# Scan of a two-layer diffusion trunk on one core: TensorE's order per group, fewer loads at the opening, and first output weights split in pieces

## The reference, cut to what matters

```python
    v = _bidir_long_conv(v * x1, h_fwd, h_bwd, f_bias)
    return (v * x0) @ out_w
```

```python
    y_diag = jnp.einsum('bclsgr,bcsgrp->bclgrp', cb[..., None] * decay, xdt)
    ...
    y_off = jnp.einsum('bclgn,bcgrpn->bclgrp', cm, starts) * jnp.exp(a_cum)[..., None]
    y = (y_diag + y_off).reshape(b, length, SSD_HEADS, SSD_HEAD_DIM)
    ...
    y = y_f + _flip(y_b) + d_skip.astype(jnp.float32)[:, None] * xh
    y = y.reshape(b, length, SSD_D_INNER) * jax.nn.silu(z.astype(jnp.float32))
    y = _rmsnorm(y, norm_g).astype(h.dtype)
    return y @ out_w, s_f, s_b
```

## Time and profile before

| | us |
|---|---|
| median of 3 runs | 3874.42 (3873.01 to 3878.49) |
| profiled execution | 3875.18 |
| its span, first to last instruction | 3873.4 |
| Hyena output, first to last product of TensorE | 851.0 to 987.3 |
| scan, first load issued to last residual | 2476.2 to 2946.0 |

### The profile page before, as it was taken

One profiled execution on the slowest core, in us unless ns is written; L12 is line 12 of the kernel. 1 busy time (PEld: TensorE's weight loads), 2 busy tenths in 40 slices (PEclk: granted clock), 3 DMA queues, 4 the chain that ended last, 5 costly groups with the idle time before them and its releaser, 6 DMA issues. The chain is left out here.

```text
span 3873.4 us, 58285 instructions
## 1 busy us (share of the span) xinstructions
PE 3469.3 (90%) x23815; PEld 2919.6 (75%) x23815; DVE 1830.3 (47%) x3029; ACT 1279.6 (33%) x2042; POOL 368.3 (10%) x355
## 2 busy tenths in 40 slices
PE   4999898979499999997899999589996499999996
PEld 2999643448399999996799999455555499999995
DVE  6233366555533333333444555678885533333333
ACT  4223312024133333333333223356665133333332
POOL 0000000000011111111010000000000011111111
PEclk6999899989699999998899999799997699999998
DMA  6556302055588888885143443676664488888885
GB/s 227 177 199 209 136 11 73 0 180 174 182 293 291 291 284 284 286 292 164 52 140 104 149 155 110 218 267 228 223 229 153 157 291 293 290 284 284 288 292 197
DMA packets 412727, 789.78 MB, mean 204 GB/s; under 512 B 22071, under 2 KB 107772, under 8 KB 412299
## 3 DMA queue, kind: packets, MB, share of 16 engines
q1 hardware_dynamic: 384012, 701.15, 51.4%
q0 software_dynamic: 28368, 86.61, 7.8%
q10 hardware_dynamic: 208, 0.10, 0.0%
HBM read 678.89 MB, written 108.90 MB: 203 GB/s over the span
## 5 line engine op out<-in xcount | busy, mean ns | idle before, releaser
L2017 PEld LDWEIGHTS moe_banks<-moe_xt,mix_ring 128*128 128x128 f32 x8192 | 1012.3, 191 | 5.5 <-issue 3.2
L2017 PE MATMUL moe_banks<-moe_xt,mix_ring 128*128 128x144 f32 x8192 | 1013.6, 287 | 3.1 <-ACT moe_xt L2052 3.1
L62 PE MATMUL ssdin_banks<-h_leading,ssdin_w_split 128*128 128x384 f32 x1920 | 412.0, 344 | 0.0
L2039 PE MATMUL moe_banks<-moe_down_parts,moe_hid_parts 128*128 128x512 f32 x1536 | 357.6, 392 | 0.0
L2097 DVE TENSOR_TENSOR moe_hid<-moe_banks,moe_sg 128x128 f32<-128x128 f32 x256 | 74.6, 292 | 581.8 <-ACT moe_sg L2075 581.8
L62 PEld LDWEIGHTS ssdin_banks<-h_leading,ssdin_w_split 128*128 128x128 f32 x1920 | 337.1, 188 | 14.4 <-issue 13.6
L2039 PEld LDWEIGHTS moe_banks<-moe_down_parts,moe_hid_parts 128*128 128x128 f32 x1536 | 285.8, 188 | 71.4 <-issue 13.2
L2087 DVE TENSOR_TENSOR moe_down_parts<-mix_ring,moe_down_parts 128x2048 fp32r<-128x2048 f32 x128 | 292.2, 2283 | 0.0
L2975 PE MATMUL scan_banks<-scan_w,scan_yc 128*128 128x512 f32 x576 | 256.5, 599 | 0.0
L62 PE MATMUL hyin_banks<-h_leading,hyin_w_split 128*128 128x384 f32 x1152 | 238.2, 338 | 11.5 <-DVE hyin_w_split L751 11.5
L1984 POOL DMA_INDIRECT x_dram<-moe_yc,mix_idx_quarter x128 | 167.6, 1309 | 809.3 <-DVE moe_yc L2108 780.1
(11 more groups left out here) (412 smaller groups left out, 4368.8 us busy)
## 6 DMA issues: line engine op xcount, KB each, us to landing
mix_ring<-in_moe_w_gate SPq DMA_DIRECT2D x64, 2048.0 KB, 7.8
mix_ring<-in_moe_w_up SPq DMA_DIRECT2D x64, 2048.0 KB, 12.7
mix_ring<-in_moe_w_down SPq DMA_DIRECT2D x64, 2048.0 KB, 15.8
early_ring<-in_ada_w SPq DMA_DIRECT2D x96, 512.0 KB, 5.8
scan_cum<-row_dram SPq DMA_DIRECT2D x36, 1024.0 KB, 6.3
ssd_w<-in_ssd_in_w SPq DMA_DIRECT2D x40, 512.0 KB, 4.1
scan_states<-s_dram SPq DMA_DIRECT2D x36, 512.0 KB, 7.6
s_dram<-ssdin_work SPq DMA_DIRECT2D x64, 256.0 KB, 2.0
```

What stands on the lines that cost most here:

```text
L62: ins = pe.matmul(out(piece), w_at(w[a], k), h_k(h[b], k, piece), start=(k == 0 and a == 0 and b == 0), stop=(k == KD - 1 and a == 1))
L2017: ins = pe.matmul(pb[:, 2 * (f % 2) + j, 0:SLOTS], ring[:, 2 * half + j, k, col:col + P], xt[:, k, :], start=(k == 0), stop=(k == KD - 1))
L2039: ins = pe.matmul(pb[:, LAT_BANK[half], :], hid_parts[:, a, k, :], wd[:, half, b, k, :], start=(k == 0 and a + b == 0), stop=(k == KD - 1 ...
```

## The change

In the scan TensorE's round becomes: the states' products of n, `cb(n + 1)`, `project(n - 1)`, the mixing products of n. Since two sets of products that lie apart in time now add to the same PSUM bank, each group first writes zeros to the whole bank by a product of one row of zeros (`y_open`), and all others only add. The row of zeros is copied once by ScalarE. The states of tile 0 are no longer loaded (they aren't used), so the group's semaphore counts 48 for the first four groups. The gate and x tile 0 are issued behind the load of group 6, gate and x tile 1 behind that of group 8. In the Hyena output each weight half is prepared in four pieces of two k rows; TensorE waits for each piece of the second half apart.

```diff
@@ phase_hyena_out
+        W_PIECES = 4
+        def weight_piece(half, piece):
+            return slice(2 * piece, 2 * piece + 2), slice(half * HALF, (half + 1) * HALF)
         def lead_count(t):
-            return t + 3 if t else 2
+            return 2 * W_PIECES + t + 1 if t else W_PIECES + 1
...
                     act.wait_ge(s_w[half], 16)
-                    act.activation(w_parts[:, 0, :, cols], w[:, :, cols], ACT.Copy).then_inc(s_hi, 1)
+                    for piece in range(W_PIECES):
+                        ks, cols = weight_piece(half, piece)
+                        act.activation(w_parts[:, 0, ks, cols], w[:, ks, cols], ACT.Copy).then_inc(s_hi, 1)
...
-                    elif t == 0:
-                        pe.wait_ge(s_lo, 3)
                     for k in range(KD):
+                        if t == 0 and half and k % 2 == 0:
+                            pe.wait_ge(s_lo, piece_count(1, k // 2))
...
@@ phase_scan
-                    sp.dma_start(sg[:, r, :, :], io["s_dram"][max(t, 1), :, g, :, :]).then_inc(s_in[r], 16)
+                    if t:
+                        sp.dma_start(sg[:, r, :, :], io["s_dram"][t, :, g, :, :]).then_inc(s_in[r], 16)
...
-                    if n == 3:
-                        for c in range(2):
-                            sp.dma_start(gate[:, c, :], io["vec_dram"][1, c, V_G1:V_G1 + 1, :].partition_broadcast(P)
-                                         ).then_inc(s_gate, 16)
-                        load_x(0)
-                        load_x(1)
+                    if n in (6, 8):
+                        c = CTX if n == 6 else LATENT
+                        sp.dma_start(gate[:, c, :], io["vec_dram"][1, c, V_G1:V_G1 + 1, :].partition_broadcast(P)
+                                     ).then_inc(s_gate, 16)
+                        load_x(n // 2 - 3)
...
+                def y_open(n):
                     if n >= 2:
                         pe.wait_ge(s_yk, 4 * (n - 1))
+                    pe.matmul(pb[:, y_bank(n), :], zero[0:1, :], zero[0:1, :].unsqueeze(1).broadcast_to([1, 4, P]),
+                              start=True, stop=False)
...
+                def y_states(n):
+                    t, r, b = n // GROUPS, n % RING, n % 2
+                    y_open(n)
+                    if t:
+                        pe.wait_ge(s_ce, n - GROUPS + 1)
+                        y_terms(n, [(sg[:, r, d, :], ec[:, b, d * GH:(d + 1) * GH, :]) for d in range(2)], False)
+                def y_mix(n):
+                    r, b = n % RING, n % 2
+                    pe.wait_ge(s_mix, n + 1)
+                    y_terms(n, [(xdt[:, b, d, :], cum[:, r, d, :, :]) for d in range(2)], True).then_inc(s_y, 1)
...
                 for n in range(N + 2):
                     if n < N:
-                        y(n)
+                        y_states(n)
                     if n + 1 < N:
                         cb(n + 1)
                     if 1 <= n <= N:
                         project(n - 1)
+                    if n < N:
+                        y_mix(n)
```

More of the change, by code:

```diff
@@ L1448, in phase_hyena_out, with piece_count @@
         s_cur = m.sem("affinities_cleared")
+        W_PIECES = 4
+        def weight_piece(half, piece):
+            return slice(2 * piece, 2 * piece + 2), slice(half * HALF, (half + 1) * HALF)
         def lead_count(t):
-            return t + 3 if t else 2
+            return 2 * W_PIECES + t + 1 if t else W_PIECES + 1
+        def piece_count(half, piece):
+            return half * (W_PIECES + 1) + piece + 1
         with nc.Block() as block:
@@ L1493, in lead @@
                         act.wait_ge(s_mm, t - 1)
-                        act.wait_ge(s_lo, t + 1)
+                        act.wait_ge(s_lo, lead_count(t - 2))
                     act.activation(g_parts[:, t % 2, 0, :, :], g[:, t % G_RING, :, :], ACT.Copy).then_inc(s_hi, 1)
                 for half in range(2):
-                    cols = slice(half * HALF, (half + 1) * HALF)
                     act.wait_ge(s_w[half], 16)
-                    act.activation(w_parts[:, 0, :, cols], w[:, :, cols], ACT.Copy).then_inc(s_hi, 1)
+                    for piece in range(W_PIECES):
+                        ks, cols = weight_piece(half, piece)
+                        act.activation(w_parts[:, 0, ks, cols], w[:, ks, cols], ACT.Copy).then_inc(s_hi, 1)
                     if half == 0:
@@ L1559, in rest_of_weights @@
                 def rest_of_weights(half):
[L1560 to L1563, removed]
+                    for piece in range(W_PIECES):
+                        ks, cols = weight_piece(half, piece)
+                        dve.wait_ge(s_hi, piece_count(half, piece))
+                        dve.tensor_tensor(w_parts[:, 1, ks, cols], w[:, ks, cols], w_parts[:, 0, ks, cols].bitcast(F32), ALU.subtract
+                                          ).then_inc(s_lo, 1)
                 def rest(t):
@@ L2864, in phase_scan @@
         ones = m.sb("ones", [P, 2])
+        zero = m.sb("zero", [1, P], F32R)
         xr = m.sb("x", [P, 2, D])
@@ L2876, in phase_scan @@
         s_one = m.sem("ones_ready")
+        s_null = m.sem("zeros_ready")
         s_gw = m.sem("w_scaled")
@@ L2907, in out_bank, with group_in @@
             return (3, 6)[t % 2]
-        def heads(d, g):
-            return slice(d * HEADS + g * GH, d * HEADS + (g + 1) * GH)
+        def group_in(n):
+            return sum(48 if k < GROUPS else 64 for k in range(n % RING, n + 1, RING))
         with nc.Block() as block:
@@ L2959, in cb @@
                     r = n % RING
-                    pe.wait_ge(s_in[r], 64 * (n // RING + 1))
+                    pe.wait_ge(s_in[r], group_in(n))
                     if n:
@@ L2977, in project, with y_terms @@
                     ins.then_inc(s_pj, 1)
[L2979 to L2983, removed]
+                def y_open(n):
                     if n >= 2:
                         pe.wait_ge(s_yk, 4 * (n - 1))
[L2986 to L2990, removed]
+                    pe.matmul(pb[:, y_bank(n), :], zero[0:1, :], zero[0:1, :].unsqueeze(1).broadcast_to([1, 4, P]),
+                              start=True, stop=False)
+                def y_terms(n, terms, last):
+                    for i, (left, right) in enumerate(terms):
+                        for j in range(4):
                             for half in range(2):
@@ L2994, in y @@
                                                 left[:, h * HEAD:(h + 1) * HEAD], right[:, h, :],
-                                                start=(i == 0), stop=(i == len(kinds) - 1))
-                    ins.then_inc(s_y, 1)
+                                                start=False, stop=(last and i == len(terms) - 1 and j == 3))
+                    return ins
+                def y_states(n):
[8 more added lines that the diff above has]
+                    y_terms(n, [(xdt[:, b, d, :], cum[:, r, d, :, :]) for d in range(2)], True).then_inc(s_y, 1)
                 def norm(t):
@@ L3004, in _ @@
                 pe.wait_ge(s_one, 1)
+                pe.wait_ge(s_null, 1)
                 cb(0)
@@ L3048, in root @@
                                    ).then_inc(s_rt, 1)
+                act.activation(zero[0:1, :], tri[0:1, TRI_GT, :], ACT.Copy).then_inc(s_null, 1)
                 for n in range(N + 3):
@@ L3072, in prepare @@
                     t, g, r, b = n // GROUPS, n % GROUPS, n % RING, n % 2
-                    dve.wait_ge(s_in[r], 64 * (n // RING + 1))
+                    dve.wait_ge(s_in[r], group_in(n))
                     if n >= 2:
@@ L3117, in residual @@
                     dve.wait_ge(s_pj, 4 * t + 4)
-                    if t == 0:
-                        dve.wait_ge(s_gate, 32)
-                    else:
+                    if t < 2:
+                        dve.wait_ge(s_gate, 16 * (t + 1))
+                    if t:
                         dve.wait_ge(s_sum, t)
```

## The result

The changed kernel takes 3882.0 us in the median of 20 runs (3874.64 to 3885.55), the kernel before 3875.51 beside it (20 runs, 3873.01 to 3878.99). The ratio is 1.0016, 95% interval 1.0009 to 1.0022: +6.2 us, with 3.5 to 8.5 as the interval. The forecast was +3.9 us, no change that counts, on the slow side; the time lies in the range of 3869 to 3888. The interval excludes zero, so the kernel did get slower, by 6.2 us where the prediction took 7.7 as the least that counts.

What follows compares the result with a forecast made beforehand. VectorE and ScalarE's ring was taken to bound the scan, with TensorE in slack, and TensorE's start the Hyena output. Scan 9.2 - 1.5 - 1.5 = +6.2, weights -2.3, sum +3.9: 3878.3 us, range 3869 to 3888.

Steps and rivals of the forecast that it cites:

- the ring: Scan: closed ring of VectorE and ScalarE from one gated product to the next sets the pace; tile 48.79 us.
- The short step: Even stretch of the scan: shortest step per tile grows from 9.65 to 10.96 us, seven times, +9.2 us.
- The opening: Scan's first groups: fewer and later loads, but TensorE's chain is late in their place; net -1.5 us.
- G(1): End of group 1's gated product in the scan (G(n) for group n); forecast at 2518.4, before 2512.91.
- The tail: Scan's end: last projection ends at 2940.99 instead of 2942.74, 1.7 us earlier, taken as -1.5 us.
- The output weights: Start of Hyena output projection: weight halves in pieces let TensorE start at 848.75 instead of 851.02, -2.3 us.
- a later rise of its clock eats it: Hyena output projection: end of the bounds in which the earlier TensorE start gains 0 us.
- The queue of SyncE: Scan: loads waiting behind the moved gates and x tiles are needed a whole step later; cost zero.
- The low clock gets into the new chain: Rival, scan: low clock slows projection plus mixing between two gated products; 3883.7 to 3888.8 us, named 3885; chance 0.25.
- TensorE's waits are the bound: Rival, scan: TensorE's 29.6 us of waits for the mix are the path and are won back; 3842.5 us; chance 0.04.
- The opening gives what the bytes say: Rival, scan's opening: mixing follows DMA, not the projections, saving 10.4 us instead of 1.5; 3869.4 us; chance 0.10.
- The short step doesn't grow: Rival, even stretch of the scan: shortest step stays near 9.65 us, 9.2 us fall out; 3869.1 us; chance 0.08.

Runs made afterwards that it cites:

- the order alone: Kernel before with only TensorE's new scan order and its zero row, loads and output weights as before: 3891.0 us, ratio 1.0038.
- the context's old order: Changed kernel with the projection last again in the four rounds of the context tile only: 3874.41 us, ratio 0.9999 against before.
- the new order with early decays: Changed kernel, with ScalarE making the start decays of group n+1 before it squares group n-1: 3848.21 us, ratio 0.9928.
- the start decays: Kernel before with changed loads and weight pieces, old TensorE order; ScalarE makes start decays of group n+1 before squaring group n-1: 3823.46 us, ratio 0.9865.
- the loads alone: Kernel before with only the scan's loads changed (no states for tile 0, gates and x tiles 0 and 1 later): 3865.08 us, ratio 0.9972.
- half the projection: Changed kernel with every second product of the scan's output projection left out: 3855.21 us in one run.
- the first five kernels: Before with only new order 3891.0, only loads 3865.08, only weight pieces 3872.5, loads plus pieces 3861.19; changed kernel with old order in context rounds 3874.41 us.

## Why the prediction was right

**What bounds the scan.** Right. The reading "TensorE is in the ring only by products that are long done" was tested from both sides: filling TensorE's waits gave nothing and cost 15 us by itself; taking one instruction out of the ring gave 38. It gave no more because TensorE's slack, 43.7 of 48.79 us a tile by the prediction, was then used up.

**The size.** The time came nearer than its parts. The scan was forecast at +6.2 us and came at +9.9; from the first copy of output weights to the scan's first load -2.3 was forecast and -3.7 came, so 1.4 of the scan's miss was cancelled there by luck.

**The short step.** Forecast 10.96, measured 11.01 to 11.09; seven of them +9.2, and the stretch measured +9.9. The terms were 0.16 + 6.96 + 1.97 + 0.04 + 1.83; the first is 0.19 and the last 1.85 in the trace shown. (What the prediction calls 32 products in 1.97 us are 32 records, of 16 products; the time is right.) The count, the places and the unchanged steps of 14.57, 12.65 and 11.92 were right, and so was the zero product's cost of nothing: it takes 0.49 us in the trace, the forecast's bound from one record was 0.25 to 0.50, and it stands where TensorE has time to spare.

**The opening.** Right in kind, mis-sized in one term. G(1) was forecast 5.5 us later than before and came 6.9 later; G(4) 1.5 earlier and came 0.3 earlier. Of the 1.2 missing, 1.07 is the first projection: I took 8.7 us and it took 9.77, still inside the bounds of 7.03 and 14.1. Another 0.3 of G(1)'s miss is its start, 30.0 us after the first load where I had 29.7. I had put the low clock at a third of the window, read from before; but with the new order TensorE has still less to do there ahead of the projection, 4.90 us of idle time right before it, and the clock rose later. I let the change alter the work and kept the clock of the old work.

**The tail.** The step that failed: -1.5 forecast, +0.3 measured. The chain alone was right, as the order alone shows with -1.7. What it left out is the clock: 8.83 instead of 7.13 us, in the changed kernel, in the one with the context's old order and in the new order with early decays, but not in the one with the order alone. All four have the same 1.95 us of idle time ahead; what makes the difference stays open.

**The output weights.** Start -2.35, forecast -2.3. The stage gave some 0.8 more in the means of the profiles (1.4 in this pair), and 0.5 of it is a shorter start at the low clock. I had bounded a loss there ("a later rise of its clock eats it") and found the reverse.

**The queue of SyncE.** Zero, as said: with the loads moved, all steps behind G(4) are those of before, to 0.02 us.

**The rivals.** "The low clock gets into the new chain" came half true: it took 1.1 us in the opening and 1.7 in the tail, together short of the 3.8 us from which I had said that it decides. In the even stretch it cost nothing that shows: of the 36 windows of 10 us from 2560 to 2920 five have a mean of 0.83 (before: two of 0.83, one each of 0.90 and 0.93), all in a tile's longest step, where TensorE waits and has 3.6 us in hand, and no short step is over 11.1. "TensorE's waits are the bound" is refuted. By the Trainium skill ("Perfetto Trace Analysis", Optimization Strategies) the goal is a TensorE as busy as can be; here it was busier, 3490.0 against 3469.3 us, and the kernel slower; but most of the added time is the 36 zero products of about 0.5 us, which are no work of the model. The same section's second sentence, to optimise the engine that blocks it, is what the start decays did, and the trace agrees: TensorE then has no idle time from 2540 to 2890. "The opening gives what the bytes say" needed G(1) no later than 2512, and that is what the loads alone have and the changed kernel has not. "The short step doesn't grow" holds, among the kernels with the new order, only with half the projection.

**The expectations of the parts** came out within 2 us in the time for the first five kernels, for the order alone with errors that cancelled. For the early decays I was 4.5 us too slow with the old order, where I had put the tile at 44.4 to 44.6 and it is 43.84. With the new order I was 2.8 too slow, though the tile came as expected (46.2, measured 46.35); where those 2.8 lie isn't shown.

## What to carry to other kernels

A long wait of the busiest engine is not yet time to be won: ask first whether its product is late for the one who reads it. If the readers' own ring sets the pace, a job moved into the wait gains nothing, and it costs as soon as it stands between two links of the ring. Then look in that ring for an instruction that is queued behind a wait that it doesn't need itself; here that was one line of ScalarE, worth six times what the change cost. The gain ends where the next bound stands, here a TensorE without idle time.

## What the runs showed of the hardware that I had not expected

- A product of one row of zeros over 512 columns (L2997) takes 0.49 to 0.50 us in the records at the full clock, and 0.79 at the low one.
- Executions of two kernels with the same 1.95 us of idle time before the last projection ran it in 7.13 us (order alone) and in 8.83 us (changed kernel), the second at a mean granted clock of 0.81.
- Splitting an instruction of 128x4096 in four pieces cost 3.90 us for 3.62 on ScalarE and 4.63 for 4.43 on VectorE, and TensorE's first product came 2.35 us sooner.
